# Experts ranked by load: 12 in units of their own, 52 in pairs on the two column halves of TensorE, with the expert loop written out

## The chip, the cores and the metric

The kernel runs on one core of one Trainium2 chip. The metric is device time in microseconds of one launch, the median of several runs. Each launch computes one trunk layer for 128 context tokens and 256 latent tokens, all in fp32.

## The reference, cut to what matters

The layer is a mixer (attention and a scan) and then a mixture of experts over all 384 tokens. The change touches only the second. Each token goes to 6 of 64 experts, an expert has a gate and an up matrix of 1024 x 256 and a down matrix of 256 x 1024, and one shared expert of the same size sees every token:

```python
scores = jax.nn.sigmoid((x2 @ p['router_w']).astype(f32))
biased = scores + p['router_b'].astype(f32)
...
_, eidx = lax.top_k(jnp.where(emask > 0, biased, -jnp.inf), TOP_K)
wsel = jnp.take_along_axis(scores, eidx, axis=-1)
wsel = wsel / jnp.sum(wsel, axis=-1, keepdims=True) * ROUTED_SCALE
...
def expert(acc, e):
    wg, wu, wd, ge = e
    y = (jax.nn.silu(x2 @ wg) * (x2 @ wu)) @ wd
    return acc + ge[:, None] * y, None
```

So there are 384 x 6 = 2304 rows of 1024 numbers to be sent to experts, 36 an expert on average. An expert's weights are 2,048 KB (gate and up side by side, `w13`) and 1,024 KB (down, `wd`).

## The kernel before

The program is written engine by engine, with semaphores between them: `sp` issues plain DMAs, `pool` (GpSimd) issues indirect ones, `pe` is TensorE, `act` and `dve` are ScalarE and VectorE. The first half of the time is the mixer, which the change leaves alone. Then:

**Routing.** VectorE makes the one-hot choice `oh` and the mask `emask` of each token (L1178 to L1184) and then the gate values (L1185 to L1192). Meanwhile TensorE sums the masks into each row's position in its expert (`positions`, L1609). VectorE turns position and expert into a slot number (L1194 to L1201): slot = 64 x position + expert. GpSimd scatters the 18 columns of records (row, token, gate value) to a list in DRAM by slot number (L512), clears four token buffers (L519) and reads the list back (L522). The first 128 positions of an expert are its list; what is beyond goes through a block that runs only when a flag is set (`If(flag > 0)`).

**The expert stage.** For each of the 64 experts, always with 128 slots whatever it has to do:

- `sp` loads its weights into one of four slots of SBUF (`load_expert`, L412). Expert e waits until the down projection of expert e-4 is done (L428).
- `pool` gathers its tokens from DRAM into one of four buffers `xg` (`gather`, L529), and scatters its result rows (`scatter`, L554). In the loop the order is gather for e+3, then scatter of e (L572 to L576).
- `pe` runs gate/up of e as 8 accumulating matmuls of 128 tokens by 512 columns (`up`), the 8 transposes of the tokens of e+1 (`tokens_t`), the down projection of e-1 (`finish`: 4 matmuls by 512), and the 2 transposes of the hidden layer of e (`hid_t`), in this order (`expert`, L1659). In fp32 each matmul is two instructions in the trace, each transpose one.
- `act` and `dve` move the results out of PSUM, half each: `tokens_t`, `hidden`, `hidden_t`, `out_half`. `out_half` multiplies by the gate value and is what `scatter` waits for.

Experts 0 to 3 and 60 to 63 are written out, the others are a loop on each engine over groups of four. All engines take the experts in the order 0 to 63. Loads 2 and 3 are issued once the shared expert is done and the first gather has landed (L420 to L424).

**The end.** When the last scatter has landed (L444), six rows per token are read back and summed, and the layer's output is written.

Of the kernel before, what the change touches and what calls it, by code (L numbers as in the profile page):

```python
# [7 lines left out]
F32 = mybir.dt.float32  # L20
# [24 lines left out]
NB = E_N // 4  # L45
OVER = P * E_N
# [97 lines left out]
def program(nc, A, O):  # L144
    ctx = ExitStack()
    with ctx:
# [108 lines left out]
        slot_at = [21552, 0, 12288, 27696]  # L255
# [9 lines left out]
        xg = [ar(s, D) for s in (6144, 7168, 18480, 19504)]  # L265
        xgT = [ar(8192 + D * i, D).rearrange("p (c t) -> p c t", c=KC) for i in range(2)]
        yb = [ar(10240 + D * i, D) for i in range(2)]
# [6 lines left out]
        lists = ar(39600, 768).bitcast(I32).rearrange("p (b e w) -> p b e w", b=3, e=E_N)  # L274
# [17 lines left out]
        ix = [ar(41844 + 4 * i, 4).bitcast(I32) for i in range(4)]  # L292
        gx = [ar(43024 + 4 * i, 4).bitcast(I32) for i in range(4)]
# [6 lines left out]
        def gate(u):  # L300
            return ix[u][:, 2:3].bitcast(F32)

        yk_d = nc.dram_tensor("expert_rows", [T * TOP_K, D], F32).ap()
        list_d = nc.dram_tensor("slot_lists", [T * E_N, 4], I32).ap()
# [18 lines left out]
        def _(sp):  # L323
# [49 lines left out]
            for t in range(TT):  # L373
                sp.dma_start(res[:, t, :], A["x"][t * P:(t + 1) * P, :]).then_inc(sem("d_mb"), 16)
            for i, n in enumerate(("lnx_g", "lnx_b")):
                sp.dma_start(lnx[:, i, :], A[n].partition_broadcast(P)).then_inc(sem("d_lnx"), 16)
# [22 lines left out]
            sp.dma_start(slot13[3], A["shared13"]).then_inc(sem("d_shared"), 16)  # L399
            sp.dma_start(slotd[3], A["shared_wd"]).then_inc(sem("d_shared"), 16)  # L400
            sp.dma_start(slot13[0], A["w13"][0]).then_inc(sem("d_we0"), 16)
            sp.dma_start(slotd[0], A["wd"][0]).then_inc(sem("d_we0"), 16)
# [9 lines left out]
            def load_expert(u, e, it):  # L412

                sp.dma_start(slot13[u], A["w13"][e]).then_inc(sem(f"d_we{u}"), 16)
                sp.dma_start(slotd[u], A["wd"][e]).then_inc(sem(f"d_we{u}"), 16)


            load_expert(1, 1, 0)
# [3 lines left out]
            sp.wait_ge(sem("d_xg0"), 16)  # L422
            load_expert(2, 2, 0)
            load_expert(3, 3, 0)  # L424
            with sp.Fori(1, NB) as it:
                for u in range(4):

                    sp.wait_ge(sem("dn_ps"), it * 4 + (u - 3))  # L428
                    load_expert(u, it * 4 + u, it)
# [3 lines left out]
            with sp.If(flag > 0):  # L433
                sp.wait_ge(sem("dn_ps"), E_N)
                for b in range(2):
# [7 lines left out]
            sp.wait_ge(sem("dn_ps"), E_N)  # L443
# [17 lines left out]
        def _(pool):  # L461
# [50 lines left out]
            for k in range(TT * TOP_K):  # L512
                pool.indirect_dma_start(out=list_d, out_offset=bass.IndirectOffsetOnAxis(ap=desti[:, k:k + 1], axis=0),
                                        in_=rec[:, k, :], in_offset=None, bounds_check=T * E_N - 1,
                                        oob_is_err=False).then_inc(sem("d_list"), 16)

            pool.wait_ge(sem("h2"), TT)
            pool.wait_ge(sem("route"), 5)
            for b in range(4):  # L519
                pool.memset(xg[b], 0.0).then_inc(sem("zero"), 1)  # L520
            pool.wait_ge(sem("d_list"), 16 * (TT * TOP_K + 1))
            pool.dma_start(lists, list_d.rearrange("(b p e) w -> p b e w", b=3, p=P)).then_inc(sem("d_list"), 16)  # L522
            pool.wait_ge(sem("d_list"), 16 * (TT * TOP_K + 2))
            pool.wait_ge(sem("d_h2"), 48)
            pool.wait_ge(sem("zero"), 9)
            n_ix = sem("ix")
            last_token, last_row = pool.to_reg(T - 1), pool.to_reg(T * TOP_K - 1)

            def gather(u, e, first):  # L529

                if not first:

                    pool.wait_ge(sem("xt2"), e - 3)
                    pool.sem_inc(sem("go"), 1)
                pool.tensor_copy(gx[u], lists[:, 0, bass.ds(e, 1), :].rearrange("p e w -> p (e w)")).then_inc(n_ix, 1)  # L535
                pool.wait_ge(sem("d_h2"), 48)
                pool.wait_ge(n_ix, e + 1 if isinstance(e, int) and e < 3 else e * 2 - 1)
                if not first:

                    pool.wait_ge(sem("xt2"), e - 3)  # L540
                pool.sem_inc(sem("go"), 1)
                pool.indirect_dma_start(out=xg[u], out_offset=None, in_=h2_d,  # L542
                                        in_offset=bass.IndirectOffsetOnAxis(ap=gx[u][:, 1:2], axis=0),
                                        bounds_check=last_token, oob_is_err=False).then_inc(sem(f"d_xg{u}"), 16)

            def rows(u, e, it, first):

                if not first:

                    pool.wait_ge(sem(f"d_sc{u}"), 16 * it)  # L550
                    pool.sem_inc(sem("go"), 1)
                pool.tensor_copy(ix[u], lists[:, 0, bass.ds(e, 1), :].rearrange("p e w -> p (e w)")).then_inc(n_ix, 1)

            def scatter(u, e):  # L554
                pool.wait_ge(sem("d_list"), 16 * (TT * TOP_K + 2))
                pool.wait_ge(n_ix, e * 2 + 4)
                pool.wait_ge(sem("yv"), e + 1)
                pool.wait_ge(sem("ya"), e + 1)
                pool.sem_inc(sem("go"), 1)
                pool.indirect_dma_start(out=yk_d, out_offset=bass.IndirectOffsetOnAxis(ap=ix[u][:, 0:1], axis=0),  # L560
                                        in_=yb[u % 2], in_offset=None, bounds_check=last_row,
                                        oob_is_err=False).then_inc(sem(f"d_sc{u}"), 16)


            for u in range(3):
                gather(u, u, True)
            rows(0, 0, 0, True)
            for u in range(4):
                gather((u + 3) % 4, u + 3, u == 0)
                rows((u + 1) % 4, u + 1, 1, u < 3)  # L570
                scatter(u, u)
            with pool.Fori(1, NB - 1) as it:  # L572
                for u in range(4):
                    gather((u + 3) % 4, it * 4 + (u + 3), False)
                    rows((u + 1) % 4, it * 4 + (u + 1), it + (1 if u == 3 else 0), False)
                    scatter(u, it * 4 + u)  # L576
            for u in range(4):
                if u == 0:
                    gather(3, E_N - 1, False)
                else:  # L580
                    pool.wait_ge(n_ix, 2 * (E_N - 4 + u) + 4)
                    pool.sem_inc(n_ix, 1)
                if u < 3:
                    rows(u + 1, E_N - 3 + u, NB - 1, False)
                scatter(u, E_N - 4 + u)
            for u in range(4):
                pool.wait_ge(sem(f"d_sc{u}"), 16 * NB)
            pool.wait_ge(sem("route"), 8)
            flag = pool.value_load(flagi[0:1, 0:1], min_val=0, max_val=1)  # L589
            with pool.If(flag > 0):  # L590
                for b in range(2):
                    with pool.Fori(0, E_N) as e:
                        n = e + b * E_N
                        pool.tensor_copy(ix[0], lists[:, b + 1, bass.ds(e, 1), :].rearrange("p e w -> p (e w)")
# [5 lines left out]
                                                in_offset=bass.IndirectOffsetOnAxis(ap=ix[0][:, 1:2], axis=0),  # L600
# [4 lines left out]
                        pool.indirect_dma_start(out=yk_d, out_offset=bass.IndirectOffsetOnAxis(ap=ix[0][:, 0:1], axis=0),  # L605
# [8 lines left out]
        def _(act):  # L614
# [192 lines left out]
            def silu(u, e):  # L807
                act.wait_ge(sem("gu_ps"), e + 1)
                if not (isinstance(e, int) and e < 2):
                    act.wait_ge(sem("hid"), e - 1)  # L810
                act.activation(sgl[u % 2], ps[:, 2 + u % 2, 0:FF], ACT.Silu).then_inc(sem("sg"), 1)  # L811

            def tokens_t(u, e):

                act.wait_ge(sem("xt2"), e + 1)
                if not (isinstance(e, int) and e < 2):
                    act.wait_ge(sem("gu_ps"), e - 1)
                act.activation(xgT[u % 2][:, 4:8, :].rearrange("p c t -> p (c t)"), ps[:, 1, :], ACT.Copy  # L818
                               ).then_inc(sem("xta"), 1)

            def out_half(u, e, it):

                act.wait_ge(sem("dn_ps"), e + 1)
                act.wait_ge(sem("ix"), e * 2 + 4)
                if not (isinstance(e, int) and e < 2):

                    act.wait_ge(sem(f"d_sc{(u + 2) % 4}"), 16 * (it + (1 if u >= 2 else 0)))
# [9 lines left out]
            def expert(u, e, it, last=False):  # L837
                silu(u, e)
                if not last:
                    tokens_t((u + 1) % 4, e + 1)  # L840
# [936 lines left out]
```

## Time and profile before

| what | us |
|---|---|
| median of 3 runs (lowest, highest) | 1582.32 (1574.39, 1588.87) |
| profiled execution, span | 1576.5 |
| TensorE busy | 1390.1 |
| VectorE busy | 472.7 |
| ScalarE busy | 289.6 |
| GpSimd busy | 222.1 |

All of it is one profiled execution. The 40 slices of its page are 39.4 us each; a digit is the busy share in tenths. PEclk is the granted clock of TensorE in tenths, and a view by windows gives it as a share (1.00 is 2.4 GHz, 0.50 is 1.2 GHz). The mean over the span was 0.931. "DMA to landing" is the time from the start of the issuing instruction until the transfer's semaphore was raised.

### The profile page before, as it was taken

The numbers are of one execution on the slowest core, as the hardware profiler recorded it, in microseconds if no ns is written. First come the engines' busy times: TensorE is split into PE (matmuls) and PEld (weight loads), VectorE is DVE, ScalarE is ACT, GpSimd is POOL, SyncE is SP. The second block draws the span as 40 slices with busy tenths as digits, with TensorE's granted clock in tenths as the row PEclk, the third lists the DMA queues.
The fourth block names the chain that finished last, engine by engine and source line by source line (L and its number), as shares of the span: only waits on it lengthen the run. The fifth ranks groups of instructions, "written<-read, shape, count | busy, mean of one in ns | idle before, by whom it ended". The sixth has DMA issues, their size and how long they took to land.

```text
span 1576.5 us, 16055 instructions
## 1 busy us (share of the span) xinstructions
PE 1390.1 (88%) x5749; PEld 813.8 (52%) x5749; DVE 472.7 (30%) x847; ACT 289.6 (18%) x582; POOL 222.1 (14%) x336
## 2 busy tenths in 40 slices
PE   6899998468999989785799999999999999999970
PEld 1155443248999989643244545454544545454530
DVE  1123394854252163445111111111111111111117
ACT  1011321231212112122111111111111111111111
POOL 0100001600000000000612121222212121212210
PEclk9899997689999889896889999999999999999995
DMA  7790200000010100343068777787878787777816
GB/s 280 274 382 1 83 25 4 1 1 1 1 56 23 54 1 2 133 169 121 11 266 311 295 297 304 291 309 289 315 285 314 295 310 298 298 300 294 319 70 277
DMA packets 64543, 290.10 MB, mean 184 GB/s; under 512 B 20816, under 2 KB 21328, under 8 KB 46944
## 3 DMA queue, kind: packets, MB, share of 16 engines
q1 hardware_dynamic: 44832, 269.63, 44.9%
q0 software_dynamic: 19664, 19.82, 3.7%
q8 instruction: 32, 0.52, 0.1%
q14 instruction: 15, 0.12, 0.0%
HBM read 300.44 MB, written 37.57 MB: 214 GB/s over the span
## 4 chain that ended last, share of the span: by engine, by line
PE 47%; DVE 2%; DMA 1%; issue 0%; SPq 0%; POOLq 0%; ACT 0%; DVEq 0%; ACTq 0%
PE ps L1291 42%; PE ps L1294 5%; DMA arena<-expert_rows 1%; DVE arena L1266 1%; DVE arena L1273 0%; DVE early L1275 0%; DMA arena<-h_scratch,arena 0%; DMA expert_rows<-arena 0%; DVE arena L1225 0%; SPq L452 0%; DVE arena L1235 0%; SPq L449 0%; POOLq L589 0%; DVE small L1272 0%; ACT arena L834 0%
## 5 line engine op out<-in xcount | busy, mean ns | idle before, releaser
L1291 PE MATMUL ps<-arena 128*128 128x512 f32 (+5 forms) x4272 | 1130.5, 431 | 27.6 <-ACT arena L714 8.0
L1291 PEld LDWEIGHTS ps<-arena 128*128 128x128 f32 (+2 forms) x4272 | 628.4, 196 | 432.1 <-issue 365.1
L1294 PEld LDWEIGHTS ps<-const,arena 128*128 128x128 f32 x1161 | 160.5, 180 | 146.5 <-issue 117.8
L1294 PE MATMUL ps<-const,arena 128*128 128x128 f32 x1161 | 176.0, 292 | 68.0 <-DVE arena L1035 28.0
L1217 DVE TENSOR_TENSOR arena<-arena,ps 128x256 f32<-128x256 f32 x64 | 26.9, 421 | 428.5 <-ACT arena L811 421.8
L560 POOL DMA_INDIRECT expert_rows<-arena x64 | 64.6, 1010 | 532.1 <-DVE arena L1235 479.0
L1291 PE MATMUL ps<-arena,small 128*2 128x512 f32 x192 | 89.8, 628 | 21.9 <-DMA adarow<-in_adarows 21.9
L1235 DVE TENSOR_SCALAR arena<-ps,arena 128x512 f32<-128x512 f32 x64 | 48.0, 751 | 186.5 <-PE ps L1291 186.5
L811 ACT ACTIVATE arena<-ps 128x256 f32<-128x256 f32 x64 | 24.5, 384 | 389.5 <-PE ps L1291 389.5
L828 ACT ACTIVATE arena<-ps,arena 128x512 f32<-128x512 f32 x64 | 44.0, 687 | 191.2 <-PE ps L1291 191.2
L542 POOL DMA_INDIRECT arena<-h_scratch,arena x64 | 66.6, 1040 | 54.8 <-POOL arena L535 47.5
L1291 PEld LDWEIGHTS ps<-arena,small 128*2 128x2 f32 x192 | 16.4, 88 | 93.2 <-issue 78.6
L738 ACT ACTIVATE arena<-ps 128x512 f32<-128x512 f32 x72 | 38.7, 595 | 124.5 <-PE ps L1294 124.5
L1064 DVE TENSOR_TENSOR arena<-ps,const 128x512 f32<-128x512 f32 x36 | 24.9, 691 | 82.6 <-PE ps L1291 82.6
L1225 DVE COPY arena<-ps 128x512 f32<-128x512 f32 x64 | 44.1, 689 | 11.8 <-PE ps L1294 9.4
L818 ACT ACTIVATE arena<-ps 128x512 f32<-128x512 f32 x64 | 38.2, 597 | 39.3 <-PE ps L1294 39.3
L949 DVE SCALAR_TENSOR_TENSOR arena<-ps,col,arena 128x127 f32<-128x127 f32 (+1 forms) x60 | 25.0, 416 | 57.4 <-ACT arena L651 55.8
L508 POOL TENSOR_TENSOR arena<-arena 128x256 f32<-128x256 f32 x1 | 0.7, 723 | 270.8 <-ACT arena L797 270.8
L466 POOL DMA_DIRECT2D mod_scratch<-modrow x12 | 6.7, 559 | 225.3 <-DVE modrow L913 163.9
L1070 DVE TENSOR_TENSOR arena<-arena,ps 128x512 f32<-128x512 f32 x36 | 24.8, 689 | 39.5 <-PE ps L1291 39.5
L1291 PE MATMUL ps<-arena,early 64*128 64x384 f32 (+3 forms) x64 | 22.9, 558 | 5.1 <-DVE arena L1006 2.4
L1266 DVE TENSOR_TENSOR arena<-arena 128x1024 f32<-128x1024 f32 x18 | 22.1, 1225 | 15.9 <-DMA arena<-expert_rows 15.3
(182 smaller groups left out, 543.4 us busy)
## 6 DMA issues: line engine op xcount, KB each, us to landing
arena<-in_w SPq DMA_DIRECT2D x64, 2048.0 KB, 8.0
arena<-in_wd SPq DMA_DIRECT2D x64, 1024.0 KB, 10.5
arena<-in_w_ada SPq DMA_DIRECT2D x12, 2048.0 KB
arena<-expert_rows SPq DMA_DIRECT2D x6, 1536.0 KB, 16.9
arena<-in_w_in SPq DMA_DIRECT2D x3, 2560.0 KB, 17.7
arena<-in_w_out SPq DMA_DIRECT2D x2, 2048.0 KB, 7.7
arena<-mod_scratch SPq DMA_DIRECT2D x8, 512.0 KB, 11.2
arena<-in_w_in SPq DMA_DIRECT2D x1, 3072.0 KB, 24.6
```

Of the source, the lines that this page charges most:

```text
L542: pool.indirect_dma_start(out=xg[u], out_offset=None, in_=h2_d, in_offset=bass.IndirectOffsetOnAxis(ap=gx[u][:, 1:2], axis=0), bounds_chec ...
L560: pool.indirect_dma_start(out=yk_d, out_offset=bass.IndirectOffsetOnAxis(ap=ix[u][:, 0:1], axis=0), in_=yb[u % 2], in_offset=None, bounds_ ...
L738: act.activation(Y[d][:, 4 * par:4 * par + 4, :].rearrange("p u t -> p (u t)"), ps[:, 4 * d + 2 + par, :], ACT.Copy).then_inc(sem("t_ev"), 1)
L818: act.activation(xgT[u % 2][:, 4:8, :].rearrange("p c t -> p (c t)"), ps[:, 1, :], ACT.Copy).then_inc(sem("xta"), 1)
L828: act.activation(yb[u % 2][:, 512:1024], ps[:, 6, :], ACT.Copy, scale=gate(u)).then_inc(sem("ya"), 1)
L949: ins = dve.scalar_tensor_tensor(out=zs[:, j, a:e], in0=b[:, a + off:e + off], scalar=cc(m + j), in1=zs[:, j, a:e], op0=ALU.mult, op1=ALU.add)
L1217: dve.tensor_tensor(hid[u % 2], sgl[u % 2], ps[:, 2 + u % 2, FF:2 * FF], ALU.mult).then_inc(sem("hid"), 1)
L1225: dve.tensor_copy(xgT[u % 2][:, 0:4, :].rearrange("p c t -> p (c t)"), ps[:, 0, :]).then_inc(sem("xtv"), 1)
L1235: dve.tensor_scalar(yb[u % 2][:, 0:512], ps[:, 5, :], gate(u), None, ALU.mult).then_inc(sem("yv"), 1)
L1266: ins = dve.tensor_tensor(ysh[:, t, :], ysh[:, t, :], yk[t][:, k * D:(k + 1) * D], ALU.add)
L1291: return pe.matmul(out, lhsT, rhs, start=start, stop=stop, skip_group_check=True)
L1294: return pe.transpose(out, in_, ident[0:n, 0:n])
```

## The change

1. The experts are ranked by their number of rows, on the chip. Experts 0 to 3 have fixed ranks 0 to 3 (`N_STATIC`). Ranks 0 to 11 have a unit each with 128 slots. Ranks 12 to 63 form 26 pairs (12+i, 38+i): one unit, slots 0 to 63 for one expert, 64 to 127 for the other. That makes 38 units (`UNITS`): the four static ones, then eight times three pairs and a single, then two pairs.
2. In a pair, a matmul has 64 token columns, and the two experts' matmuls alternate, one to PSUM partitions 0 to 63, the other to 64 to 127.
3. Weights go to five slots (`NSLOT`), `w13` and `wd` with their own semaphores and waits. From the fifth load on the expert's number is read from SBUF (`expert_at`).
4. Token buffers `xg` are two instead of four. The order on GpSimd is gather of n+2, then scatter of n. The records are used in place from `lists`; the copies `gx` and `ix` go.
5. The loops over groups of four are written out on all engines.
6. The routing gets the counts (six more matmuls), the ranks, the bases and capacities of the units, and a slot number made of main and overflow part.

```diff
+N_STATIC, N_SINGLE = 4, 12
+N_PAIR = (E_N - N_SINGLE) // 2
+N_UNIT = N_SINGLE + N_PAIR
+NSLOT = 5
...
+    plan = [(r,) for r in range(N_STATIC)]
+    single, pair = N_STATIC, 0
+    while pair < N_PAIR:
+        for _ in range(3):
+            if pair < N_PAIR:
+                plan.append((N_SINGLE + pair, N_SINGLE + N_PAIR + pair))
+                pair += 1
+        if single < N_SINGLE:
+            plan.append((single,))
+            single += 1
...
+            def load_expert(j, e):
+                k = j % NSLOT
+                if j >= NSLOT:
+                    sp.wait_ge(sem("gu_ps"), LOADS[j - NSLOT][0] + 1)
+                sp.dma_start(slot13[k], A["w13"][e]).then_inc(sem(f"d_w13{k}"), 16)
+                if j >= NSLOT:
+                    sp.wait_ge(sem("dn_ps"), LOADS[j - NSLOT][0] + 1)
+                sp.dma_start(slotd[k], A["wd"][e]).then_inc(sem(f"d_wd{k}"), 16)
...
             sp.wait_ge(sem("shared_ps"), TT)
             sp.wait_ge(sem("d_h2"), 48)
-            sp.wait_ge(sem("d_xg0"), 16)
...
+            load_expert(3, 3)
+
+            sp.wait_ge(sem("order"), 1)
+            for j in range(N_STATIC, E_N):
+                r = LOADS[j][1]
+                load_expert(j, sp.value_load(expert_at[0:1, r:r + 1], min_val=0, max_val=E_N - 1))
...
+            def gather(n):
+                if n >= 2:
+                    pool.wait_ge(sem("xt2"), n - 1)
+                u = UNITS[n][0]
+                pool.indirect_dma_start(out=xg[n % 2], out_offset=None, in_=h2_d,
+                                        in_offset=bass.IndirectOffsetOnAxis(ap=lists[:, u, 1:2], axis=0),
+                                        bounds_check=last_token, oob_is_err=False).then_inc(sem(f"d_xg{n % 2}"), 16)
+
+            def scatter(n):
+                pool.wait_ge(sem("yv"), n + 1)
+                pool.wait_ge(sem("ya"), n + 1)
...
+            gather(0)
+            gather(1)
+            for n in range(N_UNIT):
+                if n + 2 < N_UNIT:
+                    gather(n + 2)
+                scatter(n)
...
+            dve.wait_ge(sem("route"), 4)
+            own(dve.scalar_tensor_tensor(out=keyr, in0=ps[0:E_N, 1, 192:256], scalar=64.0, in1=ranks_c[0:E_N, 0:E_N],
+                                         op0=ALU.mult, op1=ALU.add))
...
+            dve.tensor_scalar(ahead, keyr, keyc, None, ALU.is_lt).then_inc(sem("rank"), 1)
+            dve.wait_ge(sem("rank"), 2)
...
+            dve.tensor_copy(expert_at, ps[0:1, 7, 0:E_N]).then_inc(sem("order"), 1)
...
+                for c in range(KC):
+                    for i in range(2):
+                        r = slice(64 * i, 64 * i + 64)
+                        ins = mm(ps[r, 2 + n % 2, :], xgT[n % 2][:, c, r], s13(at[i] % NSLOT)[:, c, :],
+                                 c == 0, c == KC - 1)
+                ins.then_inc(sem("gu_ps"), 1)
...
+            tokens_t(0)
+            for n in range(N_UNIT):
+                up_unit(n)
+                if n + 1 < N_UNIT:
+                    tokens_t(n + 1)
+                if n:
+                    down_unit(n - 1)
+                pe.wait_ge(sem("hid"), n + 1)
+                hid_t(4, hid[n % 2], "at2")
+            down_unit(N_UNIT - 1)
```

## Rows read from the trace of the kernel before

**Rows 1.** The page: the span, and the DMA share by slices in tenths
```profile
span 1576.5 us, 16055 instructions
...
DMA  7790200000010100343068777787878787777816
```

**Rows 2.** Groups by shape (busy, mean ns | idle before), and the waits of SP's queue
```profile
L1291 PE MATMUL ps<-arena 128*128 128x512 f32 x1704 | 761.9, 598 | 10.3 <-DMA arena<-in_w_out 7.9 <-DVE arena L1225 1.1 <-ACT arena L834 0.8
...
SPq L414 <- PE ps L1291: 629.3, 60, 22.8
```

**Rows 3.** Timeline of one expert: start, duration, engine, line, what, idle before
```profile
1008.89 7.03 PE L1291 MATMUL ps<-arena 128*128 128x512 f32 x16
...
1009.03 0.75 DVE L1235 TENSOR_SCALAR arena<-ps,arena 128x512 f32<-128x512 f32 x1 [2.91 <-PE ps L1291]
...
1010.60 1.01 POOL L560 DMA_INDIRECT expert_rows<-arena  x1 [8.14 <-DVE arena L1235]
...
1012.63 1.04 POOL L542 DMA_INDIRECT arena<-h_scratch,arena  x1 [0.82 <-POOL arena L535]
...
1015.76 1.05 PE L1294 MATMUL ps<-const,arena 128*128 128x128 f32 x8
...
1016.64 3.60 PE L1291 MATMUL ps<-arena 128*128 128x512 f32 x8
...
1020.48 0.75 DVE L1235 TENSOR_SCALAR arena<-ps,arena 128x512 f32<-128x512 f32 x1 [2.94 <-PE ps L1291]
```

**Rows 4.** By windows, while two experts' weights are in flight; last: clock, DMA share, GB/s
```profile
790.00:804.00 14.00, 12.87 (x36) 6.85 (x36) 1.81 (x3) 1.91 (x4) 2.55 (x5) 0.77 0.99 397
```

**Rows 5.** The line of the gathers, all 64
```profile
L542 POOL DMA_INDIRECT arena<-h_scratch,arena x64: 1016/1042/1091, 786.3 to 1491.9; - x64
...
DMA to landing us min/median/max: 3.3/8.0/12.0
```

**Rows 6.** The same line, the third and the fourth gather each by itself
```profile
L542 POOL DMA_INDIRECT arena<-h_scratch,arena x1: 1016/1016/1016, 790.4 to 790.4; - x1
...
DMA to landing us min/median/max: 9.8/9.8/9.8
...
L542 POOL DMA_INDIRECT arena<-h_scratch,arena x1: 1016/1016/1016, 792.5 to 792.5; - x1
...
DMA to landing us min/median/max: 12.0/12.0/12.0
```

**Rows 7.** Matmuls of one attention product, 347.0 to 349.5: duration, first and last start
```profile
L1291 PE MATMUL ps<-arena x12: 378/379/431, 347.3 to 348.9; 128*64 128x256 f32 x12
```

**Rows 8.** Two idle stretches of TensorE in the timeline, then windows behind them (columns above)
```profile
714.50 1.94 PE L1294 MATMUL ps<-const,arena 128*128 128x128 f32 x8 [7.01 <-ACT arena L786]
...
789.74 0.45 PE L1294 MATMUL ps<-const,arena 128*128 128x128 f32 x1 [7.84 <-DMA arena<-h_scratch,arena]
...
714.50:718.00 3.50, 3.50 (x17) 3.50 (x18) 2.18 (x2) 1.54 (x3) 0.00 (x0) 0.50 0.14 54
718.00:721.00 3.00, 3.00 (x26) 2.86 (x26) 0.00 (x0) 0.00 (x0) 0.00 (x0) 1.00 1.09 358
...
789.70:796.40 6.70, 5.81 (x13) 3.37 (x14) 0.69 (x1) 0.60 (x1) 2.55 (x5) 0.50 0.92 345
```

**Rows 9.** Timeline of the routing: positions, slot numbers, their conversion and maximum
```profile
745.57 2.82 PE L1291 MATMUL ps<-arena,const 128*128 128x64 f32 x12 [10.30 <-DVE arena L1180]
...
749.81 0.36 DVE L1195 SCALAR_TENSOR_TENSOR arena<-ps,arena 128x192 f32<-128x192 f32 x1
...
753.82 0.16 DVE L1203 TENSOR_REDUCE arena<-arena 128x1 f32<-128x18 f32 x1
```

**Rows 10.** Timeline: the evictions of experts 0, 61 and 63
```profile
814.81 0.75 DVE L1235 TENSOR_SCALAR arena<-ps,arena 128x512 f32<-128x512 f32 x1 [2.75 <-PE ps L1291]
...
1511.13 0.75 DVE L1235 TENSOR_SCALAR arena<-ps,arena 128x512 f32<-128x512 f32 x1 [2.75 <-PE ps L1291]
...
1526.41 0.75 DVE L1235 TENSOR_SCALAR arena<-ps,arena 128x512 f32<-128x512 f32 x1 [4.00 <-PE ps L1291]
```

More of the change, by code:

```diff
@@ L44, with unit_order @@
 BIG = 1 << 20
-NB = E_N // 4
-OVER = P * E_N
+N_STATIC, N_SINGLE = 4, 12
+N_PAIR = (E_N - N_SINGLE) // 2
+N_UNIT = N_SINGLE + N_PAIR
+OVER = P * N_UNIT
+N_LIST = OVER + T * E_N
+NSLOT = 5
+def unit_order():
+    plan = [(r,) for r in range(N_STATIC)]
[8 more added lines that the diff above has]
+            single += 1
+    out, at = [], 0
+    for ranks in plan:
+        out.append((ranks[0], ranks, tuple(range(at, at + len(ranks)))))
+        at += len(ranks)
+    return out
+UNITS = unit_order()
+LOADS = [(n, r) for n, (_, ranks, _) in enumerate(UNITS) for r in ranks]
 C_GPRE, C_QG, C_KG, C_MP, C_MN, C_W0, C_A0, C_KK, C_KA, C_RK = 0, 8, 9, 10, 25, 40, 48, 56, 60, 64
@@ L433, in _ @@
             with sp.If(flag > 0):
[L434 to L435 removed]
+                sp.wait_ge(sem("dn_ps"), N_UNIT)
+                for b in range(3):
                     with sp.Fori(0, E_N) as e:
@@ L526, in _ @@
[L526 to L562, printed above, removed]
@@ L565, in _ @@
[L565 to L587, printed above, removed]
+            pool.wait_ge(sem("zero"), 7)
+            last_token, last_row = T - 1, T * TOP_K - 1
@@ L837, in expert @@
[L837 to L840, printed above, removed]
-                if not (isinstance(e, int) and e == 0):
-                    out_half((u + 3) % 4, e - 1, it - (1 if u == 0 else 0))
-                hidden_t(u, e)
-            tokens_t(0, 0)
-            for u in range(4):
-                expert(u, u, 0)
-            with act.Fori(1, NB - 1) as it:
-                for u in range(4):
-                    expert(u, it * 4 + u, it)
@@ L851, in _, with silu, tokens_t @@
-            for u in range(4):
-                expert(u, E_N - 4 + u, NB - 1, last=u == 3)
-            out_half(3, E_N - 1, NB - 1)
+            def silu(n):
+                act.wait_ge(sem("gu_ps"), n + 1)
+                if n >= 2:
+                    act.wait_ge(sem("hid"), n - 1)
+                act.activation(sgl[n % 2], ps[:, 2 + n % 2, 0:FF], ACT.Silu).then_inc(sem("sg"), 1)
+            def tokens_t(n):
+                act.wait_ge(sem("xt2"), n + 1)
+                if n >= 2:
+                    act.wait_ge(sem("gu_ps"), n - 1)
+                act.activation(xgT[n % 2][:, 4:8, :].rearrange("p c t -> p (c t)"), ps[:, 1, :], ACT.Copy
+                               ).then_inc(sem("xta"), 1)
@@ L856, in _ @@
             with act.If(flag > 0):
-                for b in range(2):
+                for b in range(3):
                     with act.Fori(0, E_N) as e:
@@ L1228, in out_half @@
-            def out_half(u, e, it):
-                dve.wait_ge(sem("dn_ps"), e + 1)
-                dve.wait_ge(sem("ix"), e * 2 + 4)
-                if not (isinstance(e, int) and e < 2):
-                    dve.wait_ge(sem(f"d_sc{(u + 2) % 4}"), 16 * (it + (1 if u >= 2 else 0)))
-                dve.tensor_scalar(yb[u % 2][:, 0:512], ps[:, 5, :], gate(u), None, ALU.mult).then_inc(sem("yv"), 1)
-            def expert(u, e, it, last=False):
-                hidden(u, e)
-                if not last:
-                    tokens_t((u + 1) % 4, e + 1)
-                if not (isinstance(e, int) and e == 0):
-                    out_half((u + 3) % 4, e - 1, it - (1 if u == 0 else 0))
@@ L1244, in _, with hidden @@
-            dve.wait_ge(sem("sh_y"), TT)
-            tokens_t(0, 0)
-            for u in range(4):
-                expert(u, u, 0)
-            with dve.Fori(1, NB - 1) as it:
-                for u in range(4):
-                    expert(u, it * 4 + u, it)
-            for u in range(4):
-                expert(u, E_N - 4 + u, NB - 1, last=u == 3)
-            out_half(3, E_N - 1, NB - 1)
+            def hidden(n):
+                dve.wait_ge(sem("sg"), n + 1)
+                if n >= 2:
+                    dve.wait_ge(sem("at2"), n - 1)
+                dve.tensor_tensor(hid[n % 2], sgl[n % 2], ps[:, 2 + n % 2, FF:2 * FF], ALU.mult
+                                  ).then_inc(sem("hid"), 1)
@@ L1254, in _ @@
+            dve.wait_ge(sem("sh_y"), TT)
+            tokens_t(0)
+            for n in range(N_UNIT):
+                hidden(n)
+                if n + 1 < N_UNIT:
+                    tokens_t(n + 1)
+                if n:
+                    out_half(n - 1)
+            out_half(N_UNIT - 1)
             dve.wait_ge(sem("route"), 8)
@@ L1256, in _ @@
             with dve.If(flag > 0):
-                for b in range(2):
+                for b in range(3):
                     with dve.Fori(0, E_N) as e:
@@ L1674, in finish @@
-            def finish(u, e, it):
-                pe.wait_ge(sem("hta"), e + 1)
-                if not (isinstance(e, int) and e == 0):
-                    pe.wait_ge(sem("yv"), e)
-                    pe.wait_ge(sem("ya"), e)
-                down(5, hidT[u % 2], sd(u), "dn_ps")
-            tokens_t(0, 0, 0)
-            for u in range(4):
-                expert(u, u, 0)
-            with pe.Fori(1, NB - 1) as it:
-                for u in range(4):
-                    expert(u, it * 4 + u, it)
@@ new lines, in down_unit @@
+            def down_unit(n):
+                _, ranks, at = UNITS[n]
+                pe.wait_ge(sem("hta"), n + 1)
+                for j in at:
+                    pe.wait_ge(sem(f"d_wd{j % NSLOT}"), 16 * (j // NSLOT + 1))
+                if n:
+                    pe.wait_ge(sem("yv"), n)
+                    pe.wait_ge(sem("ya"), n)
+                if len(ranks) == 1:
+                    down(5, hidT[n % 2], sd(at[0] % NSLOT), "dn_ps")
+                    return
+                for hf in range(2):
+                    for c in range(2):
+                        for i in range(2):
+                            r = slice(64 * i, 64 * i + 64)
+                            ins = mm(ps[r, 5 + hf, :], hidT[n % 2][:, c, r],
+                                     sd(at[i] % NSLOT)[:, c, hf * 512:(hf + 1) * 512], c == 0, c == 1)
+                ins.then_inc(sem("dn_ps"), 1)
```

238 lines of the change are left out of this document (136 added, 102 removed).

## The prediction, made before the changed kernel was run

> **What bounds the kernel now.** I read the page first: one span of 1576.5 us, and from slice 20 on a DMA share of seven to eight tenths at about 300 GB/s [rows 1]. The groups by shape say what fills that half: 1704 records of 128x512 take 761.9 us, and the loads wait 629.3 us for TensorE, not the other way round [rows 2]. The timeline of one expert shows the period: gate/up from 1008.89 to 1015.76, eight transposes, down from 1016.64, and from one eviction of an output at 1009.03 to the next at 1020.48 about 11.42 us, with no gap on TensorE [rows 3]. 63 such periods run from the eviction of expert 0 at 814.81 to that of expert 63 at 1526.41, 711.6 us [rows 10]. So TensorE sets the expert stage. Its runner-up is the transfer of 3,072 KB an expert, 3.146 MB; the queue moved 397 GB/s at a share of 0.99 when it was full [rows 4], so an expert's weights need 7.9 us. Third is a path that is hidden today: eviction, scatter of expert e, gather of expert e+3. The gather is issued at 1012.63 and lands 8.0 us later (median, [rows 5]), but four token buffers put it nearly two periods ahead of its use.
>
> **TensorE's work.** 64 units become 38: 12 single, 26 pairs. A pair needs 32 + 16 records of 64 columns, but on two halves. Whether these overlap is shown by the attention product, which writes one column half and then the other: twelve records 128*64 by 256 start between 347.3 and 348.9, 1.6 us for eleven steps [rows 7]; a 512-wide record has a step of 0.43 us (6.87 us for 16, [rows 3]), so a 256-wide one 0.215, and eleven in a row would take 2.4 us. So the halves stream together. A pair then costs 6.87 + 0.88 + 3.43 + 0.23 = 11.4 us like a single unit, 38 x 11.42 = 434 us against 731. Bound from the other side (no overlap): 21.7 us a pair. I take overlap. The switch between halves and whole array, four times a unit, costs nothing that a row isolates; up to 0.3 us each would make 1.2, of which only the part ahead of the down projection would show below.
>
> **Transfers.** All 64 experts are still read. Pair: 6.29 MB of weights and about 61 rows of 4 KB gathered and as many scattered, 0.5 MB: 6.8/0.397 = 17.1 us. That alone would hold a pair above 11.4.
>
> **The new wait.** Two token buffers instead of four, and the GpSimd order gather(n+2), scatter(n). The gather of n+2 stands behind scatter(n-1), which waits for the eviction of unit n-1. TensorE's order is up(n+1), transposes(n+2), down(n). So each down projection waits for a gather that was issued only after the one before it. The period is the sum of a chain: eviction start to scatter start 1009.03 to 1010.60, 1.57; scatter start to gather landed, L; wake 0.15; transposes 0.88; down to the next eviction, 1016.64 to 1020.48, 3.84. Together 6.44 + L. Gate/up (6.87) lies beside L and costs nothing.
>
> L has rows on both sides. With one expert's weights in the queue: 1012.63 + 8.0 - 1010.60 = 10.0, period 16.5. With two experts' weights issued just ahead (loads 2 and 3, from 789.7): the gather issued at 790.35 took 9.8 and the one at 792.46 took 12.0, so from the first issue to the second landing 14.1 [rows 6]. In the changed kernel, which weights go out with the scatter? Load j waits for the unit of load j-5, w13 for its up, wd for its down, in program order on SP. Walking three pairs and a single: each down of a pair frees wd, w13, wd, w13 (6.3 MB) at once, the down that precedes a group's first pair frees wd, w13 (3.1 MB). So most periods are of the second kind. Rows there were 23 + 28; now about 121: 70 more rows of 4 KB at 397 GB/s, 0.7 us. The gather follows its scatter in 1.3 us instead of 2.0, but its data queue behind the scatter's, so I give nothing for it. L = 14.8, period 21.2, above the 17.1 of the transfers, so the queue is empty again before the next burst. The rule on which this turns is how a DMA engine shares itself between SP's queue and GpSimd's. The Trainium skill, DMA: Bandwidth & Descriptors, section Queues, rings and completion order, says that each engine goes round robin between its queues by whole packets, not by single descriptors. By that a scatter or gather would stand behind one weight transfer at a time: 3.3 for a gather that meets nothing [rows 5], 5.3 for a w13 (2.1 MB), 2.6 for a wd, 0.7 for rows give L 12, a period of 18.4, with the clock (below) 20.9. The two gathers of [rows 6], 9.8 and 12.0, are nearer to sharing by descriptor all along, so the sum keeps 14.8; the packet rule is a rival.
>
> **The clock.** In such a period TensorE idles from the end of up (6.8 us after the eviction) to the transposes, over 9 us. After an idle stretch of 7.01 us the granted clock was 0.50 for 3.5 us more and then 1.00 [rows 8]; after 7.8 us it was 0.50 for 6.7 us, from 789.7 to 796.4 [rows 8]. Transposes and down (4.3 us at 2.4 GHz) are exactly what runs after the gap; with 5.1 us at 1.2 GHz they take 6.9. I add 2.5 (bounds 1.7 and 3.4): 23.7 us. Periods with 3.1 MB have a gap of 4.8 us; I add nothing there (up to 2.5 each for 11).
>
> **Overflow.** Running the reference's routing on its drawn inputs gives 2304 rows, the largest experts 92, 74, 71, then 61; 12 are alone, so none overflows its 64 or 128 slots and the conditional blocks stay closed.
>
> **Start.** VectorE used 745.4 to 749.8 for gate values while TensorE made the positions (2.82 us, [rows 9]). Now it waits for positions (twelve more records, done about 751), ranks (eleven small operations of 0.2 and two trips to TensorE, 3.4), then does the gate values (4.35) and six more 128x192 operations (0.36 each, 2.2): the destinations come 11 us after 753.8. The 18 list scatters follow as before. Two clears (1.8) and the index copy (1.0) go: +8. Loads 3 and 4 no longer wait for the first gather, so list and gather 0 meet them: a gather took 9.8 instead of 3.3 [rows 5, 6]. I take 5 of that (0 to 9): +13. TensorE's positions and ranking sit ahead of the second shared gate/up, but the path through GpSimd is later.
>
> **Sum.** From the first eviction: 4 periods behind the static singles 4 x 16.5 = 66; 23 behind a 6.3 MB burst x 23.7 = 545; 7 of the 3.1 MB kind x 16.5 = 116; one with the last 4 MB, between the two kinds, 20; the last two units without a gather, as before, 1511.13 to 1526.41 = 15.3 [rows 10]. 762 against 711.6: +51. With the start +64; the end after the last scatter is unchanged. 1576.5 + 64 = 1640.5; the median of the runs lies 5.8 above the profiled span, so **1645**. Writing the loop out removes register arithmetic that no row shows TensorE waiting for: nothing. The register loads on SP (one a load) are about half a microsecond beside queued transfers: nothing.
>
> **Rivals.**
> - *The gather is fast enough* (other side). If the gather lands in 10.0 also beside a full queue, a pair runs at the 17.1 of the transfers: 66 + 23 x 17.1 + 116 + 18 + 15 = 608, 104 less, start +13: about 1490. It holds where L stays below 10.7; the sign itself turns where a burst period is (711.6 - 13 - 66 - 116 - 20 - 15.3)/23 = 20.9. For it: the median of 8.0 over 64 gathers; against: 9.8 and 12.0 in the only stretch with two experts' weights queued.
> - *Sharing by whole transfers*: a scatter waits for one w13, its gather for one wd, and no more; L 12, period 20.9, which is that turning point: about 1580, no change. This is the rule of the Trainium skill cited above.
> - *The clock costs nothing* because it stays up or comes back at once: 23 x 2.5 less, 1587, no change.
> - *The halves don't overlap*: down of a pair 6.87 instead of 3.43, on the chain: 25 x 3.4 more, 1730. Against it: the starts in [rows 7].
>
> **Chances.** Likeliest 0.50 (own range 1600 to 1690); fast gather 0.22; sharing by whole transfers or a kinder clock 0.18, of which a third comes out faster; no overlap 0.04; slower still by longer waits 0.06. The range 1480 to 1710 takes in all but the last two and a little of the first. Timing tells 1% from no change: faster 0.28, within 1% 0.11, slower 0.61.
>
> **What the profile will show.** TensorE idle before the transposes (line of `tr`), released by the gather DMA, about 9 us in two periods of three; gathers at 12 us or more; granted clock well below 1.00 in the expert stage; DMA share below 0.8; 512-wide records of 64 columns at two per 0.43 us. If instead the gathers land in 8 and the DMA share is 0.95 or more, the step that fixed L is wrong; if the clock stays at 1.00, the 2.5.

## The result

The changed kernel takes 1677.5 us (median of 4 runs, 1667.1 to 1678.1) against 1585.2 (4 runs, 1574.4 to 1588.9): ratio 1.060, 95% interval 1.056 to 1.065. It is slower, as forecast, and inside the range; the forecast was 1645. The profiled execution spans 1675.7 us.

| what, us | before | after |
|---|---|---|
| median | 1585.2 | 1677.5 |
| first eviction of an expert's output | 814.8 | 827.3 |
| last eviction | 1526.4 | 1626.0 |
| between them | 711.6 | 798.7 |
| from there to the end | 50.1 | 49.7 |

So 12.5 us are lost ahead of the first eviction and 87 us in the expert stage. In what follows a period is the time from one eviction of an output to the next. Heavy periods are the 23 in which two experts' weights (6.3 MB) are loaded, light ones the 11 with one expert's (3.1 MB). The page of after, the span and three rows of the slices in tenths (compare [rows 1]):

```profile
span 1675.7 us, 14164 instructions
...
PE   6899985579999798766776666656666566666560
...
PEclk9999986899898998968888887778877788878785
DMA  8870200000021003442446656686665766666736
```

From slice 20 on neither TensorE nor the DMA engines are full: about six tenths each. The granted clock is at seven or eight tenths, where the page of before has the highest digit, 9. When both candidates for the bound have fallen at once, something is being waited for. Two of the waits, and the landing times of the gathers (which answer to [rows 5]):

```profile
PEld ps L1290 <- DMA adarow<-h_scratch,arena: 303.8, 35, 10.3
PE ps L1290 <- DMA adarow<-h_scratch,arena: 291.3, 36, 17.8
```

```profile
L558 POOL DMA_INDIRECT adarow<-h_scratch,arena x38: 998/1019/1077, 793.1 to 1592.2; - x38
...
DMA to landing us min/median/max: 3.2/13.3/13.9
```

L1290 is the transposes, `adarow<-h_scratch` the gather. TensorE waits for it in 36 of 38 units, 291 us in all (18 of them ahead of the first eviction); the median landing went from 8.0 to 13.3 us. The timeline of one period, to be read against [rows 3]:

```profile
1012.27 1.97 PE L1290 MATMUL ps<-const,adarow 128*128 128x128 f32 x8 [8.94 <-DMA adarow<-h_scratch,arena]
1014.17 5.39 PE L1287 MATMUL ps<-arena 128*64 128x512 f32 x16
...
1019.61 0.75 DVE L1238 TENSOR_SCALAR modrow<-ps,arena 128x512 f32<-128x512 f32 x1 [4.64 <-PE ps L1287]
...
1019.83 7.03 PE L1287 MATMUL ps<-arena 128*128 128x512 f32 x16
...
1020.83 0.34 SPq L432 DMA_DIRECT2D arena<-in_w  x1
1021.16 1.00 POOL L566 DMA_INDIRECT expert_rows<-modrow,arena  x1 [21.36 <-DVE modrow L1238]
...
1022.47 1.02 POOL L558 DMA_INDIRECT adarow<-h_scratch,arena  x1 [0.30 <-issue]
...
1036.24 1.97 PE L1290 MATMUL ps<-const,adarow 128*128 128x128 f32 x8 [9.38 <-DMA adarow<-h_scratch,arena]
1038.15 5.34 PE L1287 MATMUL ps<-arena 128*64 128x512 f32 x16
```

Read from the eviction at 1019.61: scatter at 1021.16, gather right behind it, transposes only at 1036.24, TensorE idle for the 9.4 us before them. Eight transposes then take 1.97 us instead of 1.05, and a down projection of 16 records 5.34 instead of the 3.65 that it takes at full clock (at 1114.91 in the next kernel). The windows of the gap, of what follows it and of the next gate/up show why (clock, DMA share and GB/s at the end):

```profile
1003.40:1012.20 8.80, 0.00 (x0) 0.00 (x0) 0.42 (x1) 0.36 (x1) 0.00 (x0) 0.73 1.01 423
1012.20:1019.50 7.30, 7.23 (x25) 3.05 (x25) 0.69 (x1) 0.60 (x1) 0.00 (x0) 0.62 0.28 119
1019.80:1026.70 6.90, 6.90 (x18) 2.89 (x17) 0.56 (x1) 0.77 (x2) 2.03 (x2) 1.00 0.86 299
```

The clock was at 1.2 GHz for most of the work that stands behind the wait (0.62), and back at 2.4 GHz for the gate/up that nobody waits for. The DMA engines are full in the gap and nearly empty behind it.

The pairing itself does what it should. A pair's gate/up, two experts, 32 records:

```profile
1043.86 7.09 PE L1287 MATMUL ps<-arena 128*64 128x512 f32 x32
```

That is 7.09 us for twice the experts of the 7.03 us above it.

### The profile page after: what moved, and what is told of

It is laid out like the page before. It is cut to its first block and busy times, and to the rows that moved or that the text cites. A ratio compares the mean times of both kernels' runs of the same rounds, so it can differ in the third digit from the quotient of the medians.

```text
span 1675.7 us, 14164 instructions
## 1 busy us (share of the span) xinstructions
PE 1205.4 (72%) x5507; PEld 678.1 (40%) x5507; DVE 429.7 (26%) x785; ACT 239.6 (14%) x478; POOL 140.3 (8%) x154
## 2 busy tenths in 40 slices
DMA packets 57156, 290.14 MB, mean 173 GB/s; under 512 B 13472, under 2 KB 14000, under 8 KB 39536
## 5 line engine op out<-in xcount | busy, mean ns | idle before, releaser
L1287 PE MATMUL ps<-arena 128*128 128x64 f32 (+6 forms) x4272 | 915.7, 456 | 28.4 <-DMA arena<-in_w_out 8.2
L1287 PEld LDWEIGHTS ps<-arena 128*128 128x128 f32 (+2 forms) x4272 | 500.6, 186 | 387.0 <-issue 316.5
L1290 PE MATMUL ps<-const,adarow 128*128 128x128 f32 x304 | 73.0, 418 | 291.3 <-DMA adarow<-h_scratch,arena 291.3
L1290 PEld LDWEIGHTS ps<-const,adarow 128*128 128x128 f32 x304 | 58.6, 218 | 323.1 <-DMA adarow<-h_scratch,arena 303.8
L1290 PE MATMUL ps<-const,arena 128*128 128x128 f32 (+1 forms) x597 | 101.2, 310 | 61.3 <-DVE arena L1017 28.0
L1290 PEld LDWEIGHTS ps<-const,arena 128*128 128x128 f32 (+1 forms) x597 | 81.1, 170 | 106.0 <-issue 72.4
L1287 PEld LDWEIGHTS ps<-arena,small 128*2 128x2 f32 x192 | 16.3, 87 | 89.2 <-issue 76.0
L566 POOL DMA_INDIRECT expert_rows<-modrow,arena x19 | 19.0, 1001 | 376.0 <-DVE modrow L1238 376.0
L804 ACT ACTIVATE arena<-ps 128x256 f32<-128x256 f32 x38 | 14.6, 383 | 246.4 <-PE ps L1287 246.4
L566 POOL DMA_INDIRECT expert_rows<-arena x19 | 19.0, 1001 | 362.5 <-DVE arena L1238 344.0
L558 POOL DMA_INDIRECT adarow<-h_scratch,arena x38 | 38.7, 1020 | 26.5 <-issue 11.0
L1238 DVE TENSOR_SCALAR arena<-ps,arena 128x512 f32<-128x512 f32 x19 | 14.3, 751 | 84.1 <-PE ps L1287 84.1
## 6 DMA issues: line engine op xcount, KB each, us to landing
arena<-in_w SPq DMA_DIRECT2D x64, 2048.0 KB, 10.7
```

The lines of the kernel that those rows point to most:

```text
L558: pool.indirect_dma_start(out=xg[n % 2], out_offset=None, in_=h2_d, in_offset=bass.IndirectOffsetOnAxis(ap=lists[:, u, 1:2], axis=0), boun ...
L1238: dve.tensor_scalar(yb[n % 2][:, 0:512], ps[:, 5, :], lists[:, UNITS[n][0], 2:3].bitcast(F32), None, ALU.mult).then_inc(sem("yv"), 1)
L1287: return pe.matmul(out, lhsT, rhs, start=start, stop=stop, skip_group_check=True)
L1290: return pe.transpose(out, in_, ident[0:n, 0:n])
```

## The experiments

Nine kernels were run. Where an interval is given there are 4 to 10 runs beside the kernel before; the kernel with the gap filled has two runs, the others one. The runs of one kernel lie within about 1% of each other. The first ones start from the changed kernel and each differs in one thing.

**The gather ahead of the scatter.** Token buffer (n+3) mod 2 is free once the transposes of n+1 are done, which is before the down projection of n. This is the order that the kernel before had, with four buffers.

```diff
             gather(1)
+            gather(2)
             for n in range(N_UNIT):
-                if n + 2 < N_UNIT:
-                    gather(n + 2)
+                if n + 3 < N_UNIT:
+                    gather(n + 3)
                 scatter(n)
```

> One edit: GpSimd issues the gather of unit n+3 ahead of the scatter of unit n, instead of the gather of n+2. The token buffer is free by then. Theory (the down projection waits for a gather that stands behind the scatter before it): the wait of TensorE for the gathers, about 295 us, goes; periods with 6.3 MB of weights fall from 23.8 to the 17.1 of the transfers, the others from 20 to about 11.5; 23 x 17.1 + 11 x 11.5 + 15 + 15 = 550 instead of 799 from first to last eviction, total about 1430, clock back near 1.00. Rival (transfers of weights alone set the period, or the halves of the array do): within 1% of 1677.

Measured: 1421.9 us, ratio to before 0.899 (0.896 to 0.903), 10% below the kernel before and 15% below the changed one. First to last eviction 541.8 us. Issuing the gather one unit further ahead turns a loss of 6% into a gain of 10%. The expectation had 1430 and 550, and its rival falls. The gathers still take as long to land (median 13.2), but only the first is waited for. The new wait is for weights, and the DMA engines are full. The clock over the stage is 0.93, not quite the 1.00 expected, since these waits leave gaps too: the pair shown takes 9.40 us for its gate/up instead of 7.09. The page, the wait, the line of the gathers, the pair and its down projection in the timeline, and the window over most of the stage:

```profile
DMA  8692030000000210004440578999989999999936
...
PE ps L1288 <- DMA arena<-in_w: 79.7, 21, 6.8
```

```profile
DMA to landing us min/median/max: 3.2/13.2/14.8
```

```profile
1104.48 9.40 PE L1288 MATMUL ps<-arena 128*64 128x512 f32 x32 [5.61 <-DMA arena<-in_w]
...
1114.91 3.65 PE L1288 MATMUL ps<-arena 128*64 128x512 f32 x16
```

```profile
840.00:1340.00 500.00, 424.81 (x1728) 176.11 (x1727) 61.99 (x101) 64.47 (x134) 65.68 (x65) 0.93 0.95 386
```

**The gap filled.** Unused matmuls keep TensorE at work while it waits.

```diff
                 up_unit(n)
+                if 2 < n < N_UNIT - 2:
+                    for _ in range(8 if len(UNITS[n - 2][1]) == 2 else 3):
+                        mm(ps[:, 7, :], ident, const[:, 0:512])
                 if n + 1 < N_UNIT:
```

> Between gate/up and the transposes TensorE gets unused matmuls (8 fp32 ones of 512 columns where the unit two back was a pair, 3 where it was a single, into a bank that is free), so that its idle gap falls from 9.5 us to under 3. Nothing else changes. Theory (2.5 to 3 us of each period are transposes and down at 1.2 GHz): from the transposes to the eviction 4.7 us instead of 7.4, heavy periods 21.1, light ones 17.5, total 1677 - 34 x 2.6 = about 1590. Rival (the clock costs nothing on this chain): 1677 or a little above it.

Measured: 1616.3 us (1610.2 and 1622.5), first to last eviction 740.6 instead of 798.7. More work for TensorE and 61 us less time. The transposes of the heavy periods start 16.3 us after the eviction as in the changed kernel (16.4), so the gain is all behind them. The gap there is about 2 us (timeline) and the clock over the stage 0.96 instead of 0.80 (window, third number from the end):

```profile
1017.28 7.03 PE L1287 MATMUL ps<-const 128*128 128x512 f32 x16
1026.44 1.16 PE L1290 MATMUL ps<-const,adarow 128*128 128x128 f32 x8 [2.13 <-DMA adarow<-h_scratch,arena]
```

```profile
840.00:1540.00 700.00, 622.36 (x2168) 251.63 (x2170) 62.96 (x101) 65.59 (x135) 68.74 (x68) 0.96 0.71 279
```

It misses the 1590 expected because in some periods the clock still drops behind the shorter gap: from the transposes to the eviction it takes 4.8 us in some and 6.5 in others (mean 5.5, in the changed kernel 7.3). The length of the gap alone does not tell which: 6.5 us stand behind a gap of 1.9 us and 4.8 behind the gap of 2.4 in the period after it.

**A quarter of the weights, then almost none.** From the sixth expert on, only the first 4 and 2 KB of each 16 and 8 KB row are read, or only 256 bytes (64 and 64 in the edit in place of 1024 and 512). The output is not the reference's; transfers, DMA packets (57156 in each) and waits are the same.

```diff
-                sp.dma_start(slot13[k], A["w13"][e]).then_inc(sem(f"d_w13{k}"), 16)
+                a, b = (4096, 2048) if j < NSLOT else (1024, 512)
+                sp.dma_start(slot13[k][:, 0:a], A["w13"][e][:, 0:a]).then_inc(sem(f"d_w13{k}"), 16)
...
-                sp.dma_start(slotd[k], A["wd"][e]).then_inc(sem(f"d_wd{k}"), 16)
+                sp.dma_start(slotd[k][:, 0:b], A["wd"][e][:, 0:b]).then_inc(sem(f"d_wd{k}"), 16)
```

> From the sixth expert on only a quarter of each weight row is read (the rest of the slot keeps old numbers, so the output is not the reference's); order and waits are kept. Theory (the gather lands late because the weights share the DMA engines with it): landing falls from 13.3 to under 6 us, the period to 6.44 + about 6 = 12.5, total about 1677 - 799 + 37 x 12.5 = 1340. Rival (descriptor making on GpSimd is the latency): landings stay above 10, period above 17, total above 1500.

> The order of the changed kernel; from the sixth expert on only 256 bytes of each weight row are read (output not the reference's). Number of transfers, descriptors and waits are the same as with a quarter of each row, where the gathers landed after 6.8 us (median) and the kernel took 1404. Theory (what is left of the landing at a quarter is still bytes): landing 4 to 5 us, chain 6.44 + 1.3 + 4.5 = 12.2, total 799 -> 37 x 12 = 444, about 1325. Rival (what is left is the making and taking turns of descriptors): landing 6 or more, total 1390 or more.

Measured: 1403.6 us and 1311.2 us. The landing times of the gathers in the two:

```profile
DMA to landing us min/median/max: 3.3/6.8/9.4
```

```profile
DMA to landing us min/median/max: 3.2/4.3/9.6
```

13.3, 6.8 and 4.3 us for 6.3, 1.6 and 0.1 MB of weights a pair. With the scatter's 1.3 us before the gather that is an L (from the scatter's start to the gather's landing) of 14.6, 8.1 and 5.6: about 1.5 us for each MB beside a floor of 5.6. So the weights in the same DMA engines make nine of the nearly fifteen us; the rest is what the two indirect transfers take with next to nothing beside them. A quarter of the weights was expected to bring the landing under 6 and the kernel to 1340; it was 6.8 and 1404, since the remaining weights count and since gaps of 2 to 4 us still cost clock in some periods. With almost none the landing is in the 4 to 5 expected and TensorE waits at most 0.3 us before any transposes of the stage; 1325 was expected.

**No pairs.** `N_SINGLE` = 64: the order and the two buffers of the changed kernel, one expert a unit.

```diff
-N_STATIC, N_SINGLE = 4, 12
+N_STATIC, N_SINGLE = 4, 64
...
-    while pair < N_PAIR:
+    while pair < N_PAIR or single < N_SINGLE:
```

> N_SINGLE = 64: no pairs, 64 units of 128 slots, all else as in the changed kernel (two token buffers, same order on GpSimd, five weight slots, ranking). Theory (order and buffers are the loss, pairing is a gain): each unit costs a light period of about 19.5 instead of 11.4, 63 x 19.5 = 1230 from first to last eviction, total about 2100. Rival (pairing is the loss): back to 1585 + 13 for the ranking, 1600.

Measured: 2033.6 us (2100 was expected, 1600 by the rival). In the order that the change chose, pairing is worth 356 us; it had hidden most of what the order costs. The periods last 17.4 to 20.7 us, on average 19.2, but for the last few, which load nothing any more. The gathers land after 9.4 (median), and behind gaps of 4.0 to 6.6 us the transposes again take 1.97 us in most periods.

```profile
1011.54 1.97 PE L1290 MATMUL ps<-const,adarow 128*128 128x128 f32 x8 [6.11 <-DMA adarow<-h_scratch,arena]
```

**No pairs, the gather first.** Both edits together.

> No pairs (N_SINGLE = 64) and the gather of n+3 ahead of the scatter of n. With both the wait and the pairs gone this is the kernel before with the ranking, five weight slots and written-out loops. Theory (the order on GpSimd is the whole loss, the pairing the whole gain): units at 11.42 again, 1583 + 10 to 13 for the ranking = about 1595. Rival (two token buffers or the dynamic loads cost something by themselves): periods above 12, total above 1630.

Measured: 1590.4 us against 1580.4 for the kernel before in the same rounds, ratio 1.0055 (1.0027 to 1.0083). Periods are 11.4 us throughout, first to last eviction 711.1 as before (711.6), the clock 1.00. Two token buffers instead of four, five weight slots and their registers, and the written-out loops cost nothing that is seen here. What stays is the start: the first eviction is at 829.0 instead of 814.8 in the two profiles. So the loss of the changed kernel is the order, not the number of buffers.

| | one expert a unit | 26 pairs |
|---|---|---|
| gather(n+2), scatter(n) | 2034 | 1677 |
| gather(n+3), scatter(n) | 1590 | 1422 |
| the kernel before | 1580 to 1585 | |

**The halves by themselves.** Gather first and a quarter of the weights, so that only TensorE is left (output not the reference's); then the same with gate/up of a pair in two blocks, all of one half and then all of the other.

```diff
-                for c in range(KC):
-                    for i in range(2):
+                for i in range(2):
+                    for c in range(KC):
```

> Gather first and a quarter of each weight row (output not the reference's): neither the gather nor the weights can hold TensorE. Theory (the halves of the array run together, so a pair costs TensorE what a single costs): 37 periods at 11.4 to 11.8, 425 from first to last eviction instead of 542, total about 1300, clock 1.00. Rival (the halves or the mode changes cost): pairs above 12.5, total above 1330.

> As the one before, but gate/up of a pair in blocks: all 8 matmuls of the first half, then all 8 of the second. Theory (the halves overlap as far as TensorE looks ahead in its queue; the attention product's twelve records did): gate/up of a pair 7 to 10 us. If it never looks ahead past a block of 16 records: 13.7, pairs at 18.3, total 1300 + 26 x 6.9 = 1480. If the order doesn't matter: 1300.

Measured: 1312.9 and 1444.7 us. Gate/up of a pair in the one and in the other:

```profile
1007.25 7.09 PE L1289 MATMUL ps<-arena 128*64 128x512 f32 x32
```

```profile
1009.90 12.29 PE L1289 MATMUL ps<-arena 128*64 128x512 f32 x32
```

Alternating halves overlap wholly (32 records of 0.43 us in a row would be 13.7). In blocks they overlap only where the blocks meet: 12.29, some 1.4 us saved. The last four records of the first block start beside the first four of the second, all others alone. That is neither the 7 to 10 us of the expectation's theory nor its 13.7 for no overlap, but near the latter. In the kernel with alternating halves first to last eviction is 432.3 us for 37 periods, at a clock of 1.00. Four periods of three pairs and a single take 47.8 us there, four singles 45.6, so a pair costs TensorE about 0.7 us more than a single. The changes between halves and whole array are in this; no run has them alone.

**The down weights one load later.** With the gather first, weights are the bound. On SP, gate/up weights of load j now go out ahead of the down weights of load j-1, which wait for a down projection.

```diff
                 sp.dma_start(slot13[k], A["w13"][e]).then_inc(sem(f"d_w13{k}"), 16)
-                if j >= NSLOT:
-                    sp.wait_ge(sem("dn_ps"), LOADS[j - NSLOT][0] + 1)
-                sp.dma_start(slotd[k], A["wd"][e]).then_inc(sem(f"d_wd{k}"), 16)
+                if j > NSLOT:
+                    load_down(j - 1)
...
+            def load_down(j):
+                k = j % NSLOT
+                sp.wait_ge(sem("dn_ps"), LOADS[j - NSLOT][0] + 1)
+                sp.dma_start(slotd[k], A["wd"][held[j]]).then_inc(sem(f"d_wd{k}"), 16)
```

> The gather first, and on SP the gate/up weights of load j are issued ahead of the down weights of load j-1, so that they don't stand behind its wait for a down projection. In the variant with the gather first the queue moved 377 GB/s over the expert stage at a share of 0.92. Theory (weights' bandwidth is now the bound, and what is left are gaps in the queue): share 0.97 or more, stage 542 x 0.92/0.98 = 510, total 1395. Rival (the rate at a full queue is the limit): 1410 to 1425.

Measured: 1415.2 us, ratio 0.895 (0.890 to 0.900). Against the 1421.9 of the variant above that is 0.5% less, and the intervals overlap. It is the rival's number; the theory's 1395 is missed. Between 840 and 1340 us the share is 0.96 instead of 0.95, the rate 393 GB/s instead of 386. The queue was nearly full already.

## Why the prediction was right, point by point

**The chain.** It was 6.44 + L, and the timeline shows each link: 1.55 from eviction to scatter, transposes at 16.4 after the eviction in the mean of the heavy periods (L = 14.7, predicted 14.8), and the wait released by the gather. That the order on GpSimd makes it is shown with pairs (1677 against 1422) and without (2034 against 1590). L as a matter of shared DMA engines is shown by the two runs with fewer bytes, 8.1 and 5.6. The signs that the prediction named are there: gaps of about 9 us in two periods of three, landings over 12, a DMA share of 0.65 and a clock of 0.81 in the stage.

**The rule on whole transfers.** The prediction's working from the Trainium skill, DMA: Bandwidth & Descriptors, section Queues, rings and completion order, with its turns by whole packets, gave L = 12, about 1580 us. The trace has 14.7 beside a burst of two experts' weights. The window from the scatter's start to the gather's landing:

```profile
1021.16:1036.10 14.94, 5.70 (x14) 2.25 (x12) 0.42 (x1) 0.38 (x1) 2.02 (x2) 0.84 1.00 400
```

At 400 GB/s that is 6.0 MB. By the prediction's count of rows about 0.5 of it are the scatter's and the gather's, so some 5.5 MB of the burst's 6.3 went through meanwhile (an estimate), not the 3.1 of one w13 and one wd. The rows do not tell how the engines take turns, nor whether the rule fails or a packet held more than the one transfer that the prediction gave it.

**The heavy periods.** 23 of them were to take 23.7 each, 545 in all. They took 546.3.

**The clock.** 2.5 us a heavy period were predicted; from transposes to eviction the heavy periods take 7.4 us where 4.7 is the value at 2.4 GHz, so 2.7. Filling the gap gave back 61 us with the transposes starting as late as before, which shows it as a cause.

**The light periods, the term that was mis-sized.** The prediction said 16.5 for the 4 behind the static singles and the 7 behind a later single, and of the clock "I add nothing there (up to 2.5 each for 11)". They took 76.0 (19.0 each) and 139.6 (19.9 each), 34 us more than the 182 of the sum. The transposes began 11.5 to 13.8 us after the eviction instead of 11.7, which makes about 9 of the 34. Transposes and down took 6.1 to 7.7 us instead of 4.7, which makes the rest: the clock fell behind gaps of 4.4 to 6.6 us too. The row with the nearest gap had been one of 7.0 us with a fall [rows 8], but the trace of the kernel before had a nearer one, with the granted clock third from the end in the windows:

```profile
573.71 3.67 PE L1294 MATMUL ps<-const,arena 128*128 128x128 f32 x16 [4.66 <-DVE arena L1055]
...
569.00:573.70 4.70, 0.04 (x1) 0.00 (x0) 4.45 (x7) 0.00 (x0) 0.00 (x0) 0.74 0.00 0
573.70:578.00 4.30, 4.29 (x21) 4.30 (x21) 0.00 (x0) 2.38 (x4) 0.00 (x0) 0.50 0.00 0
```

All seven gaps of 3.8 to 7.9 us in that trace were followed by work at 1.2 GHz. So the upper bound was the value to take. This and one us each in the heavy periods and in the last gathered one (21.3 for 20) make the 37 us by which the stage came out longer (798.7 against 762). The distance from 1645 to 1677 is 4 us less, because the median lies only 1.8 above the profiled span here and not 5.8.

**TensorE's work.** Pairs at the cost of singles: 7.09 against 7.03 us for gate/up, as predicted, but the reading of [rows 7] was too strong. Two halves of six records that overlapped wholly would start within 5 steps, 1.1 us, and the rows have 1.6, between that and the 2.4 of a row. That product writes one half after the other, and so overlapped only where the halves meet, as the kernel with blocks did (12.29 us). It is the alternation of the two experts' matmuls that gives the whole overlap. What a pair costs beyond a single, which got nothing in the sum, is about 0.7 us and lies mostly beside the gather here.

**The start.** +13 was predicted, +12.5 measured, with terms that partly cancel. In the nine other kernels the first eviction lies between 819.8 and 830.4, so a match to half a microsecond is luck. The destinations came 19.0 us after VectorE's masks instead of 8.3, so 10.7 (predicted 11), but the masks themselves were 4 us earlier in this execution. Then the list and the first gathers met the fourth and fifth loads of weights:

```profile
793.08 1.08 POOL L558 DMA_INDIRECT adarow<-h_scratch,arena  x1 [6.47 <-DMA arena<-slot_lists]
...
801.84 1.95 PE L1290 MATMUL ps<-const,adarow 128*128 128x128 f32 x8 [17.78 <-DMA adarow<-h_scratch,arena]
```

The list took 6.5 us to arrive instead of 3.1, and gather 0 needed 8.7 instead of 3.3: 8.8 us where 5 were taken.

**The rivals.** That the gather would be fast enough fell with the landing of 13.3. Its kernel can be had all the same: with the wait out of the way the stage takes 541.8 us, near the 550 that the 17.1 us of transfers a pair add up to, and the total is 1422. That the clock costs nothing fell with the kernel with the gap filled. No overlap of the halves fell with the 7.09.

## What to carry to other kernels

When buffers are cut, write down for each one what its refill stands behind in its queue. Here a gather stood behind a scatter that needed the end of the step before, and a prefetch of nearly two periods became a wait in nearly each; issuing it one unit further ahead cost nothing. A latency on such a chain must be read under the traffic that the change will make, not at the median of today, and the clock that an idle gap costs belongs to the chain too, here also for gaps of 4.4 us. And two halves of an array are worth having only if their matmuls alternate.

## What the runs showed of the hardware

- Two column halves of the array overlap fully when their matmuls alternate (7.09 us for 32 fp32 records of 512 columns) and hardly when they come in blocks of 16 (12.29): there only four records of each block overlap.
- Unused matmuls made the kernel 61 us faster than the changed one: 740.6 instead of 798.7 in the stage, at a clock of 0.96 instead of 0.80.
- With gaps of 3.0 us the clock fell in some periods and not in others: in the run with a quarter of the weights eight transposes behind such a gap took 1.16 us in one period and 1.79 in the next. With the gap filled, transposes and down took 6.5 us behind a gap of 1.9 us and 4.8 behind one of 2.4.
- The landing of a gather grew by about 1.5 us for each MB of plain transfers queued beside it, from a median of 4.3 us at 0.1 MB to 13.3 at 6.3 MB.
